# A decoder trunk's norms: post-norm, residual, pre-norm and the MLP's first two slabs as one stage by chunks

## What is computed

```
def rms_norm(x, g):
    y = x * rsqrt(mean(x * x, axis=-1, keepdims=True) + 1e-6)
    return y * g

x = x + rms_norm(mixer(rms_norm(x, g_mix_pre)), g_mix_post)

def channel_mixer(x, g_pre, g_post, w_up, w_down):
    h = rms_norm(x, g_pre)
    y = square(relu(h @ w_up)) @ w_down
    return x + rms_norm(y, g_post)
```

## Time and profile before

| | |
|---|---|
| median of 3 runs | 3347.41 us (3345.31 to 3353.35) |
| profiled execution | 3347.18 us |
| its span, first to last instruction | 3345.3 us |
| PE busy | 2915.0 us, 87% |
| DVE busy | 1269.0 us, 38% |
| ACT busy | 809.2 us, 24% |
| mean granted TensorE clock | 0.918 |

### The profile page before, as it was taken

The page is one execution under the profiler, slowest core; times in us unless marked ns, Lnnn a source line. Parts: engine busy times, 40 slices in busy tenths (PEclk is TensorE's granted clock), DMA queues, the critical chain, the costliest instruction groups (busy, mean ns, idle before and its releaser), DMA issues. The chain is left out here.

```text
span 3345.3 us, 55580 instructions
## 1 busy us (share of the span) xinstructions
PE 2915.0 (87%) x24154; PEld 2616.5 (78%) x24154; DVE 1269.0 (38%) x1824; ACT 809.2 (24%) x1423; POOL 290.2 (9%) x239
## 2 busy tenths in 40 slices
PE   3998899985899899884999999999337999999995
PEld 2997788863677666643999999998117999999994
DVE  2143555532444344006333333332654233333334
ACT  2112444411333333012111111112132111111111
POOL 0221444320000132000000000000000000000000
PEclk7998899955999899896999999999678999999997
DMA  2110000001000254200111111110601111111111
GB/s 95 40 44 23 2 3 3 3 16 57 17 1 1 98 199 171 98 6 32 44 44 44 44 44 44 44 44 19 25 1 51 44 44 44 44 44 44 44 44 54
DMA packets 53506, 147.34 MB, mean 44 GB/s; under 512 B 21841, under 2 KB 22225, under 8 KB 52593
## 3 DMA queue, kind: packets, MB, share of 16 engines
q1 hardware_dynamic: 44144, 107.45, 10.5%
q0 software_dynamic: 9216, 37.75, 3.2%
HBM read 137.67 MB, written 7.51 MB: 43 GB/s over the span
## 5 line engine op out<-in xcount | busy, mean ns | idle before, releaser
L386 PE MATMUL ps<-h_ffn,mlp_split 128*128 128x362 f32 (+1 forms) x4608 | 769.2, 329 | 53.8 <-DVE mlp_split L555 53.8
L386 PEld LDWEIGHTS ps<-h_ffn,mlp_split 128*128 128x128 f32 x4608 | 766.7, 190 | 55.3 <-issue 55.3
L386 PE MATMUL ps<-mlp_u,mlp_split 128*128 128x362 f32 (+1 forms) x4608 | 768.2, 328 | 11.0 <-DVE mlp_u L567 11.0
L386 PEld LDWEIGHTS ps<-mlp_u,mlp_split 128*128 128x128 f32 x4608 | 761.2, 189 | 15.8 <-DVE mlp_u L567 15.8
L573 DVE TENSOR_TENSOR y<-y,ps 128x362 f32<-128x362 f32 (+1 forms) x384 | 181.2, 527 | 466.7 <-PE ps L386 466.7
L526 ACT CAST mlp_split<-mlp_raw 128x1024 fp32r<-128x1024 f32 x128 | 134.3, 1049 | 619.9 <-PE ps L386 608.1
L565 DVE TENSOR_TENSOR mlp_relu<-mlp_relu 128x1088 f32<-128x1088 f32 x64 | 82.7, 1292 | 490.0 <-ACT mlp_relu L539 490.0
L386 PE MATMUL ps<-h,in_split 128*128 128x362 f32 (+1 forms) x1440 | 242.9, 331 | 28.1 <-POOL in_split L447 28.1
L386 PEld LDWEIGHTS ps<-h,in_split 128*128 128x128 f32 x1440 | 242.6, 190 | 28.5 <-issue 28.5
L539 ACT ACTIVATE mlp_relu<-ps 128x362 f32<-128x362 f32 (+1 forms) x192 | 77.0, 474 | 530.8 <-PE ps L386 530.8
L555 DVE TENSOR_TENSOR mlp_split<-mlp_raw,mlp_split 128x1024 fp32r<-128x1024 f32 x128 | 156.0, 1219 | 15.7 <-ACT mlp_split L526 9.8
(11 more groups left out here) (392 smaller groups left out, 3267.2 us busy)
## 6 DMA issues: line engine op xcount, KB each, us to landing
mlp_raw<-w_mlp_dram SPq DMA_DIRECT2D x128, 512.0 KB, 3.2
in_raw<-w_in_dram SPq DMA_DIRECT2D x20, 512.0 KB, 3.2
x<-x_dram SPq DMA_DIRECT2D x2, 4352.0 KB, 14.7
y_dram<-x SPq DMA_DIRECT2D x1, 4352.0 KB, 11.7
out_ring<-w_out_dram SPq DMA_DIRECT2D x8, 512.0 KB, 4.0
pa_w<-w_pair_dram SPq DMA_DIRECT2D x4, 640.0 KB, 5.3
pa_rope<-rope_dram SPq DMA_DIRECT2D x1, 1088.0 KB, 5.0
ckv_dram<-z SPq DMA_DIRECT2D x1, 1088.0 KB, 10.6
```

The lines of the kernel that those rows point to most:

```text
L386: last = self.nc.tensor.matmul(out, w[:, a, k, m], rhs[:, b, rk, at:at + c], start=(start and n == 0), stop=(stop and n == 2))
```

## The change

The sums of squares leave the norms and move to where the values are made, and for each MLP the post-norm, the residual addition, the pre-norm and the first two up slabs become one stage, `entry`.

- `gemm` and `pooling`: as a product leaves PSUM, ACT squares the chunk of y, and PE adds it into bank 6 (`add_squares`), one slab behind its products. gemm's loops are written out.
- `mlp`, `entry`: root, reciprocal and spread, and ACT copies the spread factor into SBUF (`rate`). DVE then goes by chunks: scale y, add to x, form the tail of gain times x. ACT rounds gain times x to the head and squares the chunk of x. PE adds the squares into bank 7 and makes chunk k's matmuls of slabs 0 and 1 at once. The pre-norm's factor of a token is not applied to h: when all squares are in, it is rooted, inverted, spread through banks 6 and 7, copied into `rate`, and applied with the relu, which DVE takes from PSUM as `max(product, 0) * rate` in one pass. The square goes to ACT.
- `mlp`, the turns: the first begins at slab 2, and its down products are copied to y rather than added, so the memset goes; in the last turn ACT squares each finished chunk of y and PE adds it into bank 6 between the down products. First and last turn are written out, the six between are a loop.
- `between`: layer 0's MLP post-norm and the pool's pre-norm in one block, x squared chunk by chunk as it is added.
- `last_residual`: the last post-norm; each chunk of x is sent out as it is added.
- `norm` is left for pre0, q_lora and kv_lora; there DVE squares chunks 1, 3 and 6.
- The pool's ramps are loaded by a transfer of their own in `pooling`.

The core of the diff follows. The sum of squares, and what PE does in `entry`:

```
+    def add_squares(self, bank, of, k):
+
+        for q in range(4):
+            last = self.nc.tensor.matmul(self.ps[32 * q:32 * q + 32, bank, 0:QUARTER], self.c("ones", hi=32), of[:, QUARTER * q:QUARTER * q + QUARTER],
+                                         start=(k == 0), stop=(k == KC - 1))
+        return last
...
+                    def entry():
+
+                        pe.wait_ge(rooted.sem, rooted.at(1))
+                        for q in range(4):
+                            last = self.spread_row(q, q, rstd)
+                        last.then_inc(total.sem, 1)
+
+                        for k in range(KC):
+                            sums(7, k, 0)
+                            pe.wait_ge(x_tail.sem, x_tail.at(k + 1))
+                            for r in range(2):
+                                pe.wait_ge(tails.sem, tails.at(r + 1))
+                                last = slab_chunk(r, k)
+                                if k == KC - 1:
+                                    last.then_inc(product.sem, 1)
+
+                        pe.wait_ge(rooted.sem, rooted.at(2))
+                        for two in range(2):
+                            if two:
+                                pe.wait_ge(rate_out.sem, rate_out.at(2))
+                            for q in range(2):
+                                last = self.spread_row(6 + q, 2 * two + q, rstd)
+                            last.then_inc(total.sem, 1)
```

What ACT does in `entry`:

```
+                    def entry():
+                        self.mean_root(rstd, 6).then_inc(root.sem, 1)
+                        head(0, 0)
+                        act.wait_ge(total.sem, total.at(1))
+                        spread_out(0, range(4))
+                        head(0, 1)
+                        for k in range(KC):
+                            act.wait_ge(added.sem, added.at(k + 1))
+                            nc.scalar.activation(h[:, 0, k, :], x[:, k, :], ACT.Copy, scale=self.v("g_ffn_pre", KC * layer + k)).then_inc(x_head.sem, 1)
+                            if k >= 2:
+                                act.wait_ge(used.sem, used.at(k - 1))
+                            nc.scalar.activation(relu[:, k % 2, :], x[:, k, :], ACT.Square).then_inc(squared.sem, 1)
+                        act.wait_ge(used.sem, used.at(KC))
+                        self.mean_root(rstd, 7).then_inc(root.sem, 1)
+                        head(0, 2)
+                        for two in range(2):
+                            act.wait_ge(total.sem, total.at(2 + two))
+                            spread_out(6, (2 * two, 2 * two + 1))
```

What DVE does in `entry`, with `rest` the tail of gain times x, and its part of an up slab in a turn:

```
+                    def entry():
+                        dve.wait_ge(root.sem, root.at(1))
+                        nc.vector.reciprocal(rstd, rstd).then_inc(rooted.sem, 1)
+                        tail(0, 0)
+                        dve.wait_ge(rate_out.sem, rate_out.at(1))
+                        scale(0)
+                        for k in range(KC):
+                            if k + 1 < KC:
+                                scale(k + 1)
+                            add(k)
+                            if k == 0:
+                                tail(0, 1)
+                            else:
+                                rest(k - 1)
+                        rest(KC - 1)
+                        dve.wait_ge(root.sem, root.at(2))
+                        nc.vector.reciprocal(rstd, rstd).then_inc(rooted.sem, 1)
+                        tail(0, 2)
+                        dve.wait_ge(rate_out.sem, rate_out.at(3))
...
-                                dve.wait_ge(relu_done.sem, relu_done.at(g * UP + r + 1))
-                                tt(relu[:, r % 2, :], relu[:, r % 2, :], relu[:, r % 2, :], ALU.mult).then_inc(u_sq.sem, 1)
+                                dve.wait_ge(product.sem, product.at(g * TURN + r + 1))
+
+                                dve.wait_ge(u_tail.sem, u_tail.at(g * UP + r - 1))
+                                for n, (at, c) in enumerate(TILES):
+                                    last = stt(out=relu[:, r % 2, at:at + c], in0=ps[:, 3 * (r % 2) + n, 0:c], scalar=0.0, in1=rate[:, at:at + c], op0=ALU.max, op1=ALU.mult)
+                                last.then_inc(relu_done.sem, 1)
```

PE's sums in the last turn, and SP's transfers in `last_residual`:

```
+                                if squares and m:
+                                    sums(6, m - 1, KC)
...
+                    for k in range(KC):
+                        sp.wait_ge(added.sem, added.at(k + 1))
+                        sp.dma_start(self.io["y"][:, k, :], x[:, k, :]).then_inc(stored.sem, 16)
+                    sp.wait_ge(stored.sem, stored.at(16 * KC))
```

More of the change, by code:

```diff
@@ L346, in _, with sums @@
                 def _(pe):
[L347 to L353, removed]
+                    def sums(s):
+                        pe.wait_ge(squared.sem, squared.at(s + 1))
+                        self.add_squares(6, sq[:, s % 2, :], s).then_inc(used.sem, 1)
@@ L355, in _ @@
+                    for s in range(n_slabs):
+                        r = s % RING
+                        pe.wait_ge(landed[r].sem, landed[r].at(16 * (s // RING) + 16))
+                        pe.wait_ge(emptied.sem, emptied.at(s - 1))
+                        self.slab_product(pe, ring, r, rhs, 3 * (s % 2)).then_inc(product.sem, 1)
+                        if s:
+                            sums(s - 1)
+                    sums(n_slabs - 1)
                 @block.scalar
                 def _(act):
[L357 to L364, removed]
@@ L365, in _ @@
-                    act.wait_ge(emptied.sem, emptied.at(n_slabs))
+                    for s in range(n_slabs):
+                        act.wait_ge(product.sem, product.at(s + 1))
+                        for n, (at, w) in enumerate(TILES):
+                            last = nc.scalar.copy(out[:, s, at:at + w], ps[:, 3 * (s % 2) + n, 0:w])
+                        last.then_inc(emptied.sem, 1)
+                        act.wait_ge(emptied.sem, emptied.at(s + 1))
+                        if s >= 2:
+                            act.wait_ge(used.sem, used.at(s - 1))
+                        nc.scalar.activation(sq[:, s % 2, :], out[:, s, :], ACT.Square).then_inc(squared.sem, 1)
@@ L472, in mlp, with made @@
             u = self.sb(ctx, f"mlp{layer}_u", [P, 2, UP, TP], F32R)
+            rate = self.sb(ctx, f"mlp{layer}_rate", [P, TP])
+            rstd = relu[:, 1, 0:QUARTER]
+            def made(r):
+                return r + 1 if r < UP else UP + 2 * (r - UP + 1)
+            TURN = made(SL - 1)
             with nc.Block() as block:
@@ L511, in _ @@
                                 last.then_inc(product.sem, 1)
-                def made(r):
-                    return r + 1 if r < UP else UP + 2 * (r - UP + 1)
-                TURN = made(SL - 1)
+                                if squares and m:
+                                    sums(6, m - 1, KC)
+                    entry()
+                    turn(0, 2, False)
+                    with pe.Fori(1, N_FB - 1) as g:
+                        turn(g, 0, False)
+                    turn(N_FB - 1, 0, True)
+                    sums(6, KC - 1, KC)
                 @block.scalar
@@ L574, in turn @@
                                 last.then_inc(y_added.sem, 1)
                         dve.wait_ge(y_added.sem, y_added.at(g * KC + KC))
[L578 to L583, removed]
+                    entry()
+                    turn(0, 2, True)
```

287 lines of the change are left out of this document (215 added, 72 removed).

## The result

The changed kernel takes 3245.27 us (median of 4 runs, 3236.07 to 3248.09) against 3349.26 for the kernel before beside it (4 runs, 3345.31 to 3353.35): a ratio of 0.969 with a 95% interval of 0.967 to 0.971. The forecast was 3235, its range 3222 to 3260. The profiled execution is the lowest of the four, 3236.07 (span 3234.3).

The account below looks back on a forecast made before the run. The prediction saw two PE-bound MLP blocks, with norms keeping one engine at a time busy before, between and behind them. Its terms summed to 112.5 us off 3347.18, giving 3234.7, say 3235 us, range 3222 to 3260.

Parts of the forecast that it names:

- serial tail: Between the entry's last products and slab 2: second root's two spreads, ACT copies, relu pieces and hops, 4.1 us.
- Entry: Each MLP from its first root: slab 2 starts at 49.3 us instead of 90.3, a gain of 41.0 a layer.
- cold: Entry's products start after idle PE and lose 2.7 us at once.
- Between: Stage between the layers: 39.5 us against 46.9, a gain of 7.4.
- relu chain: MLP turns, slab 3's product to the last tail: 5.1 us after against 5.04, charged 1.0 over 16 turns.
- store: End of kernel: each chunk sent as its addition ends, 4.0 us against 12.6, a gain of 8.6.
- Pool: Pool's squares and sums moved early: gain 6.0 us, less 0.5 for the ramps' load, net 5.5.
- the price of a sum inside a stream: One sum of squares among PE's products: 0.6 us, with 0.51 and 0.92 as bounds.
- sums drain the array: Rival, chance 0.17: each of 33 sums in PE's way costs 0.92 us, 11 us in all, giving 3246.
- the clock in the serial tail: Ahead of slab 2: nothing charged for a clock fall; the rival, chance 0.15, had 2.7 us a layer, giving 3240.
- The gemm: Output gemm: six sums delay the last product by 3.6 us, then 3.9; 7.5 against 9.9, a gain of 2.4.
- the early norms: pre0, q_lora and kv_lora, where DVE squares some chunks: gain 1.0 us, between 0 and 5.5.

Follow-up runs that it names:

- e3_no_factor: Changed kernel with the pre-norm's token factor of both MLPs left out, and with it the entry's sums, second root and spreads: 3230.91 us.
- the filled one: Changed kernel with 14 more PE products of 240 columns, read by nobody, ahead of slab 2 in the MLP entry: 3242.01 us.

## Why the forecast held, and where it was off

The mechanism was right in every stretch but the serial tail. *Entry:* forecast 41.0 a layer, measured 40.3 and 38.9. DVE's chain delivered chunk 0 at 13.8 and 14.9 (forecast 14.4; in layer 1 the first slab's cast waited 3.43 us for its transfer), PE lost 2.1 and 2.4 cold (its first chunk took 5.34 and 5.63, the later ones 3.25; forecast 2.7), and was the bound, not DVE. *Between* and *store* came out within 0.7, and *relu chain* too: PE waited 11.7 us for mlp_u over the 16 turns, 11.0 before (forecast -1.0). *Pool:* 6.5 for 5.5; the ramps put its start off by 0.8, where 0.5 was charged.

Three terms were mis-sized. Behind the first MLP root the change won 101.2 of a forecast 109.1 us. There the three cost some 10: 5.2 for 26 sums, 4.0 for the clock, 0.9 for the tail; the pool gave back 1.0, the store 0.7, and the entry's start and its cold loss some 1.0, which leaves half a us. The median lies 10 above 3235 as the sum starts from 3347.18, and the kernel before took 3349.26 beside the changed one, 2.1 more.

The first is the price of a sum inside a stream: 0.79 to 0.80, where I chose 0.6 between 0.51 and 0.92. For all 33 sums that stand in PE's way this is 6.5 us. The attention's rows gave the streaming part correctly (0.46 to 0.51) but not the price of going in and out, 0.34, as there sums follow each other. The rival *sums drain the array* had the mechanism, and the 0.92 bound only 0.12 too much. That it came so near is luck: the four sums that it was read from the earlier trace rows begin 1.00 apart as ACT's squares let them, so their 3.67 is no price of a sum.

```profile
1523.46 0.20 PEld L272 LDWEIGHTS ps<-ffn_pre_sq,late_const 128*32 128x32 f32 x8 [0.80 <-ACT ffn_pre_sq L256]
1524.46 0.20 PEld L272 LDWEIGHTS ps<-ffn_pre_sq,late_const 128*32 128x32 f32 x8 [0.80 <-ACT ffn_pre_sq L256]
```

The Trainium skill, TensorEngine Tiling (Array Packing), Key Properties, says that a change of tiling mode drains TensorE. The trace agrees in that an insertion costs 0.34 us beside its streaming, between fp32r and between fp32 products; that this time is a drain, no row shows.

The second is the clock in the serial tail, priced at nothing: 2.7 us in layer 0 and 1.3 in layer 1 (26.75 and 25.38 against 24.06). The rival had a chance of 0.15 and 2.7 a layer. The step that failed put the 4.1 us nearer to a gap of 2.7 that kept the clock than to one of 6 that lost it, and took the spreads for activity that would help. The 2.7 was no safe mark either, as a wait of 2.4 lost the clock in one layer of e3_no_factor. In all seven profiles of kernels that keep this tail, the filled one among them, the clock fell in both layers; in the three whose PE works at full rate up to a single wait of 1.2 to 1.7 it never did.

The third is the tail's length, 4.55 for 4.1, twice: two round trips over ACT's copies of 1.5 us each.

That the profiled execution lies at 3236, so near the forecast, is chance: up to the MLP's root it won 9.7 us, and only some 3 of them are the change's. The gemm won 9.85 - 3.60 - 6 x 0.79 = 1.5 instead of 2.4 (3.60 from its last copies' end to the root), the early norms some 1.8 instead of 1.0 (the input product starts at 59.92 instead of 61.79, 0.4 of it an earlier load, and the two later norms won 0.3).

## What to carry to other kernels

Where norms stand between PE-bound blocks, begin the products by chunks as soon as the first chunk is normalised, and take a token's factor out to where the product leaves PSUM: the stage made so was worth 40 us a layer here, 17 of them by the overlap. Small matmuls of another tile shape inside a stream pay for going in and out, so collect them, and move what must follow the last product (root, spread, copies) under the last chunks, since a half-idle PE costs time and then the clock. Once such a stage is short, look at what it covered: the pool's loads, 11 us of waiting that stood in both kernels, were the largest single gain among those tried.

## What the hardware showed that I had not expected

A filler of full products did not hold the clock. In layer 0 it fell while the filler ran (0.79 over its first 1.3 us, then 0.50), in layer 1 as it began (0.50 over its first 1.3 us), and it came back within slab 2 in the one and as slab 2 began in the other. And equal single waits of 2.4 us, each behind 54 products without a gap, kept the clock in one layer and lost it in the other. The Trainium skill, TensorE: Matmul & The Clock Gate, Part 1, says that the monitor behind the clock runs freely and does not start with the kernel; that would let equal waits end differently, but no run here shows it.
